# The root of 1 - a*a in the recurrent branch: from a Sqrt on ScalarE to a power of 0.5 on GpSimd

## The reference, cut to what matters

```python
r = sigmoid(einsum(xb, w_r) + b_r); i = sigmoid(einsum(xb, w_i) + b_i)   # two directions
log_a = -LRU_C * r * softplus(-lam)
a = exp(log_a)
mult = sqrt(-expm1(2.0 * log_a))          # the root of 1 - a*a
u = i * xc * mult
h = scan(a, u)                            # h[t] = a[t] * h[t-1] + u[t]
```

## Time and profile before

| what | us |
|---|---|
| median of three runs | 677.75 (677.66 to 677.93) |
| span of the profiled execution, first to last instruction | 675.7 |
| median less span | 2.05 |
| TensorE busy in the span | 662.6 (98%) |
| VectorE busy | 531.1 (79%) |
| ScalarE busy | 403.0 (60%) |
| GpSimd busy | 73.0 (11%) |

### The profile page before, as it was taken

One profiled execution on the slowest core, in us unless ns is written; L12 is line 12 of the kernel. 1 busy time (PEld: TensorE's weight loads), 2 busy tenths in 40 slices (PEclk: granted clock), 3 DMA queues, 4 the chain that ended last, 5 costly groups with the idle time before them and its releaser, 6 DMA issues.

```text
span 675.7 us, 10962 instructions
## 1 busy us (share of the span) xinstructions
PE 662.6 (98%) x4006; PEld 592.5 (88%) x4006; DVE 531.1 (79%) x846; ACT 403.0 (60%) x677; POOL 73.0 (11%) x72
## 2 busy tenths in 40 slices
PE   7999999999999999999999999999999999999995
PEld 6998888888888878888899999999999998888884
DVE  5686648788888886873679997888777769899896
ACT  6537678788777874232565644455554455556574
POOL 0000401110222200000000000000000003314240
PEclk9999999999999999999999999999999999999999
DMA  7333202222222326334062444422444317999903
GB/s 252 121 102 102 73 11 68 68 72 68 63 71 69 120 68 236 107 125 125 10 174 67 127 125 126 120 70 64 120 124 125 124 47 173 240 273 174 169 1 124
DMA packets 83314, 75.94 MB, mean 112 GB/s; under 512 B 6415, under 2 KB 67022, under 8 KB 83278
## 3 DMA queue, kind: packets, MB, share of 16 engines
q1 hardware_dynamic: 77246, 63.93, 31.6%
q0 software_dynamic: 6016, 11.54, 9.7%
q10 hardware_dynamic: 16, 0.00, 0.0%
HBM read 73.37 MB, written 2.10 MB: 112 GB/s over the span
## 4 chain that ended last, share of the span: by engine, by line
PE 90%; DVE 4%; DMA 3%; ACT 1%; issue 1%; SPq 0%; DVEq 0%
PE ps L473 15%; PE ps L475 15%; PE ps L474 15%; PE ps L1883 10%; PE ps L1886 10%; PE ps L1885 10%; PE ps L1956 4%; PE ps L1960 4%; PE ps L1958 4%; DMA scr<-in_w_ffn_down_dram 2%; PE ps L1792 2%; PE ps L1742 1%; DMA raw<-in_w_in_dram 1%; PE ps L1739 1%; DVE w_lo L1379 1%; PE ps L1621 1%
## 5 line engine op out<-in xcount | busy, mean ns | idle before, releaser
L473 PE MATMUL ps<-hT_hi,w_lo 128*128 128x512 f32 (+1 forms) x288 | 100.3, 348 | 1.9 <-DVE hT_lo L1106 1.4
L475 PE MATMUL ps<-hT_hi,w_hi 128*128 128x512 f32 (+1 forms) x288 | 98.6, 342 | 0.0
L474 PE MATMUL ps<-hT_lo,w_hi 128*128 128x512 f32 (+1 forms) x288 | 98.6, 342 | 0.0
L317 DVE TENSOR_TENSOR w_lo<-raw,w_hi 128x1024 fp32r<-128x1024 f32 (+3 forms) x55 | 64.3, 1173 | 34.0 <-ACT w_hi L307 32.7
L1883 PE MATMUL ps<-f_hi,w_lo 128*128 128x256 f32 x320 | 90.7, 283 | 0.0
L1885 PE MATMUL ps<-f_lo,w_hi 128*128 128x256 f32 x320 | 90.6, 283 | 0.0
L1886 PE MATMUL ps<-f_hi,w_hi 128*128 128x256 f32 x320 | 90.6, 283 | 0.0
L307 ACT ACTIVATE w_hi<-raw 128x1024 fp32r<-128x1024 f32 (+3 forms) x55 | 53.7, 985 | 38.7 <-PE ps L475 36.5
L942 ACT ACTIVATE w_hi<-scr 128x1024 fp32r<-128x1024 f32 x50 | 51.9, 1056 | 37.3 <-PE ps L1886 32.9
L1886 PE MATMUL ps<-hT_hi,w_hi 128*128 128x256 f32 x240 | 68.0, 283 | 0.0
L1883 PE MATMUL ps<-hT_hi,w_lo 128*128 128x256 f32 x240 | 68.0, 283 | 0.0
(11 more groups left out here) (215 smaller groups left out, 1561.0 us busy)
## 6 DMA issues: line engine op xcount, KB each, us to landing
raw<-in_w_in_dram SPq DMA_DIRECT2D x12, 1024.0 KB
raw<-in_w_ffn_gate_dram SPq DMA_DIRECT2D x12, 512.0 KB, 4.8
raw<-in_w_ffn_up_dram SPq DMA_DIRECT2D x12, 512.0 KB, 5.1
raw<-in_w_ffn_down_dram POOLq DMA_DIRECT2D x12, 512.0 KB, 9.8
scr<-in_w_ffn_down_dram SPq DMA_DIRECT2D x11, 512.0 KB, 8.0
scr<-in_w_ffn_gate_dram SPq DMA_DIRECT2D x10, 512.0 KB, 5.2
scr<-in_w_ffn_up_dram SPq DMA_DIRECT2D x10, 512.0 KB, 6.0
raw<-in_w_out_dram SPq DMA_DIRECT2D x4, 1024.0 KB
```

Source lines behind the costliest of these rows:

```text
L317: last = nc.vector.tensor_tensor(split_view(w_lo, kind, t0 % 4), raw_view(kind, t0 // 2 % 2, t0 % 2), split_view(w_hi, kind, t0 % 4).bitca ...
L473: nc.tensor.matmul(dst, l_lo, r_hi, start=start, stop=False)
L474: nc.tensor.matmul(dst, l_hi, r_lo, start=False, stop=False)
L475: return nc.tensor.matmul(dst, l_hi, r_hi, start=False, stop=stop)
```

## The change

The Sqrt leaves ScalarE, with its wait. `decayed_input` on GpSimd now waits for `m2_ready` itself, raises `lru_m` to the power 0.5 in place, with the exponent read from a column of a new small tile (stretched over the 512 columns), signals `mult_ready`, and goes on as before. At the start GpSimd fills the small tile and takes one power of two columns. Nothing else moves.

```diff
+        phalf = sb("phalf", [P, 6])
...
+        half_made = sem("half_made")
...
             nc.gpsimd.memset(xp[:, :, LEFT + SEQ:], 0.0).then_inc(s_pad, 1)
+            nc.gpsimd.memset(phalf[:, 0:2], 0.5).then_inc(half_made, 1)
+            nc.gpsimd.memset(phalf[:, 2:4], 1.0).then_inc(half_made, 1)
+            pool.wait_ge(half_made, 2)
+            nc.gpsimd.tensor_tensor(phalf[:, 4:6], phalf[:, 2:4], phalf[:, 0:2], ALU.pow).then_inc(half_made, 1)
...
             def decayed_input(h, d, n, count):
 
+                pool.wait_ge(m2_ready, h + 1)
+                nc.gpsimd.tensor_tensor(lru_m[:, :], lru_m[:, :], phalf[:, 0:1].to_broadcast([P, SEQ]),
+                                        ALU.pow).then_inc(mult_ready, 1)
                 pool.wait_ge(ixc_ready, count)
                 pool.wait_ge(mult_ready, h + 1)
...
                     if kt == 1:
                         split_hi(act, t0 if last else t0 + 2, dt)
-                        act.wait_ge(m2_ready, h + 1)
-                        nc.scalar.activation(lru_m[:, :], lru_m[:, :], ACT.Sqrt).then_inc(mult_ready, 1)
```

## The result

The changed kernel takes 1262.22 us (median of four runs, 1261.7 to 1262.66) against 677.84 for the kernel before in the same comparison: a ratio of 1.861, 95% interval 1.8588 to 1.8633. The forecast was 772, the range 684 to 952. The sign was right, the size far off.

A forecast was written before the change was run, and what follows sets the result against it. TensorE, 98% busy, was taken as the bound. Span 675.7 plus 8 x (11.05 for the power + 0.84) less 0.97 in the last head gave 769.8; with 2.05 us around the span, 772 us, range 684 to 952.

The forecast's parts named there:

- What bounds the kernel: Whole span: TensorE, 98% busy; ScalarE's freed time is worth nothing in seven heads, 0.97 us in the last.
- The removal: On ScalarE, per head: one Sqrt of 0.632 us and two table loads of 1.283 us go, 25.6 us in all.
- T, bounded by rows: Length of GpSimd's power per head: 18 steps of 0.614 us, 11.05 us; ends 1.29 and 33.6 us.
- T: Time of one power over 128 x 512 on GpSimd, estimated at 11.05 us.
- worked element by element: Rival on GpSimd's power: worked one element at a time, over 34 us each, total above 952 us; chance 0.12.
- VectorE's work waits for GpSimd's instruction to end: In each head, VectorE's work with two SBUF operands, such as L315, stands for the whole power, delaying L1281.
- T + 0.84: TensorE's lateness per head in us: (0.14 + T) - 0.21 + 1.29 - 0.38, waiting for VectorE's L1281.
- not slower: Rival: the power blocks VectorE only while reading; up to 9.3 us hides before the scan, total 676.8 us; chance 0.13.
- The clock: Rival in the heads: TensorE's pauses of some 12 us drop its clock to 1.2 GHz, total 791 us; chance 0.28.
- the rival's first half: Clock rival, in TensorE's pause in each head: the clock falls to 1.2 GHz; whole rival's chance 0.28.
- The rival's second half: Clock rival, after each pause: slower TensorE work costs some 2.4 us a head, 19 in all; whole rival's chance 0.28.
- The cover at the start: Before the heads: GpSimd's wait of 67.62 us hides the small fills and the first power of two columns.

## Why the prediction was wrong, point by point

**What bounds the kernel: right, as far as the traces show it.** Freed time on ScalarE was costed at 0.97 us in the last head and nothing elsewhere. In the kernel without a root, with the product out of the way, these lines (L1276 there is L1271 before) lie 132.41 us apart, first head to last, against 132.59 before; from the second of them to the end of the span (674.6 us) it is 435.1 us against 436.0. So 0.2 us went in seven heads and 0.9 in the last.

```profile
107.06 0.69 DVE L1276 SCALAR_TENSOR_TENSOR scr<-store,fin_g 128x512 f32<-128x512 f32 x1 [0.62 <-ACT store L799]
...
239.47 0.69 DVE L1276 SCALAR_TENSOR_TENSOR scr<-xt,fin_g 128x512 f32<-128x512 f32 x1 [0.20 <-ACT xt L799]
```

The timed gain, 2.1 to 2.4 us, is larger than the 1.1 us between these two executions, and where the rest lies is not shown. One candidate is a view that the forecast doesn't use, the waits of the weight loads (PEld), where the kernel before stands 2.9 us for L1281 in seven pieces; in the kernel with the later product that line is absent. Which part of those waits reached the end was not measured by itself.

```profile
PEld ps L1742 <- DVE f_lo L1281: 2.9, 7, 1.4
```

**The removal: right.** Sixteen table loads and eight Sqrt gone, 23.3 us of ScalarE's busy time against 25.6 expected.

**"T, bounded by rows": wrong, the first of two steps that failed, and the one that put the time outside the range.** T was taken as 11.05 us, at most 33.6; it is 81.97. Both ends were made of passes over 512 columns, 18 or 26 of them at GpSimd's pace for a copy or a product (0.614 to 1.293 us). The price is 0.159 us a column, or 159 / (1293 / 512) = 63 two-operand passes. The count of arithmetic steps of a logarithm and an exponential was no upper bound for a routine whose inside no row shows. The rival "worked element by element", at 0.12, had the size, T over 34 us, though half the partitions, and so half the elements, took as long. Why a column costs 159 ns was not shown by any run, only that neither half of the partitions nor another exponent changes it.

**"VectorE's work waits for GpSimd's instruction to end": wrong for the power, the second step that failed.** It had L315 wait for the whole power and TensorE's eight waits of T + 0.84 fall on L1281. None of TensorE's listed waits is there now: the loss stands at the transposes and in the last head, where the late scan arrives, and the power holds VectorE up for 0.8 us of 82. The step holds for products: with one in the power's place TensorE waits on L1288 and the kernel loses 10 us. The sum's T + 0.84 gives 17 there, or 15 with the product's measured 1.09 us; it took every head alike, while the waits are seven in eight heads, 8.3 us in all and 2.0 at most. The Trainium skill (SBUF — State Buffer, Who interferes with whom) says that the side that starts first has the ports for the whole instruction; the traces agree for products and differ for this power, and the measurement decides: the block is over within 1.3 us of the power's start, and the power's end brings no second one.

**The rival "not slower" had the right mechanism, with the wrong T.** It said that the power hides up to 9.3 us and that each head loses T - 9.3 beyond. With T = 81.97 this gives 676.8 + 8 x (81.97 - 9.3) = 1258 us, 4 us from the measured 1262; the measured room is 8.8 to 8.9. Its 9.3 came from the scan of one head, and the ring that makes the loss return in each head was not in it. It was given 0.13, and its condition for a loss was worked out only up to T = 11. The two errors of the forecast, a price too low and a block too long, were of opposite sign: with the right T, its own sum would have given 676.8 + 8 x 82.81 = 1339 us.

**The clock: it fell, and cost some 2 us in all.** TensorE stands for 71 us per head, and its granted clock goes to the lower level, 1.2 GHz, in that stretch (windows of the kernel after: the first head's last work with the pause, then the rest of the ring up to the next power; columns as in the earlier trace rows, after the length):

```profile
119.00:189.75 70.75, 7.22 (x32) 5.63 (x30) 0.00 (x0) 0.00 (x0) 70.61 (x1) 0.57 0.05 15
189.75:199.34 9.59, 1.41 (x7) 1.42 (x8) 7.19 (x15) 5.56 (x16) 3.73 (x3) 0.50 0.01 2
```

That is what the Trainium skill says of an idle array (TensorE: Matmul & The Clock Gate, Part 1: The HAM clock gate), and the rival's first half. The kernel before shows it too, which the prediction overlooked, in its last 5.7 us, where TensorE has no work left:

```profile
670.00:675.70 5.70, 0.00 (x0) 0.00 (x0) 1.90 (x7) 1.51 (x4) 0.00 (x0) 0.71 0.42 160
```

The rival's second half, 2.4 us a head, is not seen: the room is 8.8 us with 64 columns, where the mean granted clock is 0.993, and 8.9 with 512, where it is 0.771. TensorE's slower work after the pause runs while the next power does. Only behind the last power nothing hides it: from 837.62 to 842.45 us eleven matmuls start some 0.43 us apart, and 0.23 from then on, some 2 us once.

```profile
840.77 0.63 PE L476 MATMUL ps<-f_lo,w_hi 128*128 128x512 f32 x1
841.20 0.63 PE L477 MATMUL ps<-f_hi,w_hi 128*128 128x512 f32 x1
...
842.67 0.39 PE L475 MATMUL ps<-f_hi,w_lo 128*128 128x512 f32 x1
842.90 0.39 PE L476 MATMUL ps<-f_lo,w_hi 128*128 128x512 f32 x1
```

**The cover at the start: right.** The first small power takes 0.73 us at 1.73, in a stretch where GpSimd then waits until 69 us:

```profile
1.73 0.73 POOL L613 TENSOR_TENSOR phalf<-phalf 128x2 f32<-128x2 f32 x1
68.97 7.45 POOL L623 TENSOR_TENSOR xt<-xt,store 128x512 f32<-128x512 f32 x4 [66.51 <-ACT xt L764]
```

## What to carry to other kernels

An operation that no row shows has no upper bound from counting its arithmetic: a single run of it on a few sizes says more than any count, and the forecast's upper end should have been far wider. Before costing a late arrival, follow the ring that it closes: here power, product, scan, row maxima, Exp, decay, power, with some 9.8 us in it besides the power. The room is a head's old length less those 9.8 us, and for a power that long the loss is T less the room. And starting an off-path GpSimd product earlier can cost more than the work that it saves: without any root the kernel was 8 us slower or 2.4 us faster, by the place of that one product beside VectorE's two-operand splits.

## What the runs showed of the hardware that was not expected

- A power of two tensors on GpSimd costs 0.159 us per column of fp32 (5.47 us for 32 columns, 81.97 for 512), the same on 64 partitions as on 128, and with the exponent 1.0 as with 0.5; a product of the same shape took 1.09 us.
- Beside that power VectorE's two-operand work in SBUF stands only at its start: in the mean of seven heads 0.77 us at 512 columns, 0.34 at 256, 0.01 at 32, and the same 0.77 beside a product of 512 columns. Later in the power, and across its end, it keeps its usual length (L1245 0.69 us, L319 1.23 us).
